# A two-layer decoder trunk on one core: identity products ahead of the last expert block's second half, and block 12's scatter ahead of the last turn

## The reference

```python
for l in range(DEPTH):
    h = rms_norm(x, norm1_g[l]) * (1.0 + sc1) + sh1
    y = even_mixer(...) if l % 2 == 0 else odd_mixer(...)
    x = x + g1 * y
    h = rms_norm(x, norm2_g[l]) * (1.0 + sc2) + sh2
    x = x + g2 * grouped_moe(h, router_w, router_b, moe_w_gu[l], moe_w_down[l])
return rms_norm(x, final_g)

def grouped_moe(...):
    probs = jax.nn.softmax((t @ router_w).astype(jnp.float32), axis=-1)
    ...
    gu = jnp.einsum('td,edf->etf', t, w_gu)
    act = jax.nn.silu(g) * u * gate_dense.T[:, :, None]
    y = jnp.einsum('etf,efd->td', act, w_down)
```

## Time and profile before

| | |
|---|---|
| median of 3 runs | 828.9 us (828.89 to 831.48) |
| profiled execution | 831.04 us, of which 829.2 us are its span |
| TensorE busy | 764.6 us, 92% of the span |
| DVE busy | 358.6 us, 43% |
| ACT busy | 172.6 us, 21% |
| mean granted TensorE clock | 0.986 of full speed |
| HBM read | 292.18 MB, 354 GB/s over the span |
| experts of layer 0 end with | the identity products at 392.9 to 395.8 us |
| experts of layer 1 end with | the last scatter at 818.8 to 820.8 us |

### The profile page before, as it was taken

The page is one execution under the profiler, slowest core; times in us unless marked ns, Lnnn a source line. Parts: engine busy times, 40 slices in busy tenths (PEclk is TensorE's granted clock), DMA queues, the critical chain, the costliest instruction groups (busy, mean ns, idle before and its releaser), DMA issues.

```text
span 829.2 us, 12109 instructions
## 1 busy us (share of the span) xinstructions
PE 764.6 (92%) x4952; PEld 398.7 (48%) x4952; DVE 358.6 (43%) x878; ACT 172.6 (21%) x423; POOL 14.8 (2%) x62
## 2 busy tenths in 40 slices
PE   4999999999999998866999999999999999998764
PEld 2557464464343332322777888864553434333221
DVE  0177982383222212202779957363663321221202
ACT  2033240441111011001300244253431111100101
POOL 2000000000000000000000000000000000000000
PEclk9999999999999999998999999999999999999979
DMA  9999999698999999999999935353978999999993
GB/s 344 389 387 384 386 387 411 272 421 331 416 409 390 432 425 425 427 425 404 386 386 368 330 123 204 128 204 122 385 262 334 424 419 407 423 427 428 429 419 160
DMA packets 67643, 295.12 MB, mean 356 GB/s; under 512 B 3200, under 2 KB 4864, under 8 KB 51968
## 3 DMA queue, kind: packets, MB, share of 16 engines
q1 hardware_dynamic: 65600, 291.16, 88.7%
q10 hardware_dynamic: 1840, 2.62, 0.9%
q0 software_dynamic: 144, 0.52, 0.2%
HBM read 292.18 MB, written 1.05 MB: 354 GB/s over the span
## 4 chain that ended last, share of the span: by engine, by line
PE 51%; issue 21%; DMA 12%; DVE 9%; SPq 4%; ACT 2%; POOL 0%; POOLq 0%; DVEq 0%; ACTq 0%
PE bank L1251 10%; DMA ring<-w_gu_dram 9%; PE bank L885 8%; DVE tail L2161 6%; PE bank L1273 4%; SPq L544 4%; PE bank L881 4%; PE bank L1078 3%; PE bank L1237 3%; PE bank L795 3%; DMA ring<-ada_w_dram 2%; PE bank L771 2%; DVE gb L1804 2%; PE bank L1012 2%; PE bank L1028 2%
## 5 line engine op out<-in xcount | busy, mean ns | idle before, releaser
L1251 PE MATMUL bank<-ring,scr 128*64 128x512 f32 (+1 forms) x992 | 195.4, 627 | 33.0 <-DMA ring<-w_gu_dram 20.5
L885 PE MATMUL bank<-hT,ring 128*128 128x256 f32 x640 | 141.6, 380 | 0.4 <-DVE hT L1892 0.4
L1251 PEld LDWEIGHTS bank<-ring,scr 128*64 128x64 f32 (+1 forms) x992 | 56.4, 132 | 155.3 <-issue 129.0
L885 PEld LDWEIGHTS bank<-hT,ring 128*128 128x128 f32 x640 | 120.6, 190 | 17.6 <-issue 1.6
L1273 PE MATMUL bank<-ring,scr 128*64 128x512 f32 (+1 forms) x544 | 102.4, 597 | 0.4 <-issue 0.4
L1804 DVE SCALAR_TENSOR_TENSOR gb<-ring,small,gb 128x512 f32<-128x512 f32 x84 | 63.2, 752 | 2.9
L881 PE MATMUL bank<-ring,hT 128*128 128x512 f32 x128 | 56.9, 598 | 0.6 <-ACT hT L1509 0.5
L2383 DVE SCALAR_TENSOR_TENSOR hT<-bank,small,gb 128x512 f32<-128x512 f32 x26 | 19.5, 751 | 87.2 <-PE bank L1273 85.7
L1273 PEld LDWEIGHTS bank<-ring,scr 128*64 128x64 f32 (+1 forms) x544 | 29.3, 127 | 54.9 <-issue 52.7
L2370 DVE TENSOR_TENSOR hT<-bank,hT 128x256 f32<-128x256 f32 x28 | 11.9, 424 | 83.9 <-ACT hT L1731 83.9
L2161 DVE SCALAR_TENSOR_TENSOR tail<-scr,col,tail 128x256 f32<-128x256 f32 x120 | 47.7, 474 | 0.0
(11 more groups left out here) (318 smaller groups left out, 772.1 us busy)
## 6 DMA issues: line engine op xcount, KB each, us to landing
ring<-w_gu_dram SPq DMA_DIRECT2D x58, 2048.0 KB, 19.0
ring<-w_down_dram SPq DMA_DIRECT2D x28, 2048.0 KB, 15.1
ring<-ada_w_dram SPq DMA_DIRECT2D x24, 2048.0 KB, 15.9
ring<-od_w_in_dram SPq DMA_DIRECT2D x9, 2048.0 KB, 19.9
ring<-ev_w_in_dram SPq DMA_DIRECT2D x5, 2048.0 KB, 19.6
ring<-w_down_dram SPq DMA_DIRECT2D x8, 1024.0 KB, 27.6
scr<-w_gu_dram SPq DMA_DIRECT2D x12, 512.0 KB, 10.7
ring<-ev_w_out_dram SPq DMA_DIRECT2D x2, 2048.0 KB, 18.2
```

The lines of the kernel that those rows point to most:

```text
L885: ins = pe.matmul(banks[h][:, m * 256:(m + 1) * 256], w[:, c, (2 * h + m) * P:(2 * h + m + 1) * P], x_part[:, c, :], start=(c == 0 and m = ...
L1251: ins = pe.matmul(b[o:o + r, :].rearrange("p (u f) -> p u f", u=2), h[:, c, r * i:r * i + r], wm, start=(first and c == 0), stop=(last and ...
```

## The change

It changes three places in the experts of both layers. On TensorE, in the loop's last round (b = 13), three identity products into bank 0 stand between the turn of the slot map and `up(13, 1)`. Behind the loop, `scatter(12)` stands ahead of `turn_act(13)` instead of behind it. On DVE, `low_y(12)` stands ahead of `activation(13)` instead of behind it. No wait, no load and no buffer is new.

```diff
@@ -1399,11 +1399,13 @@
                     if b % 2 == 1 or b == BLOCKS - 1:
                         pe.wait_ge(pg_built, built(l, b // 2))
                         slots_T(fill_t("PT", b // 2), pg[b // 2 % 2], range(2 if b % 2 else 1)).then_inc(t_full, 1)
+                    if b == BLOCKS - 1:
+                        keep_busy(3, bank[0])
                     up(b, 1)
                     if b == 0:
                         rows_of(b)
+                scatter(BLOCKS - 2)
                 turn_act(BLOCKS - 1)
-                scatter(BLOCKS - 2)
                 result(BLOCKS - 1)
                 scatter(BLOCKS - 1)
                 if l == 0:
@@ -2431,8 +2433,8 @@
                         slot_map(pcur[SLOTS_AT[b] % 2], rgs, SLOTS_AT[b])
                 slots_out(BLOCKS // 2 - 1)
                 result(BLOCKS - 2)
+                low_y(BLOCKS - 2)
                 activation(BLOCKS - 1)
-                low_y(BLOCKS - 2)
                 dve.wait_ge(flag_ready, l + 1)
                 over = dve.value_load(flag[0:1, l:l + 1])
                 result(BLOCKS - 1)
```

## The result

The changed kernel takes 833.4 us (median of 22 runs), the kernel before, beside it, 829.9 (22 runs): a ratio of 1.0032, with a 95% interval from 1.0021 to 1.0043. The means, from which the ratio comes, differ by 2.7 us (833.1 and 830.4), the medians by 3.5. Forecast were 828.8 and a range of 827.6 to 831.2. Of the distance from 828.8 to 833.4, 1.0 us is the kernel before itself, whose median over 22 runs is 829.9 where the three runs that the forecast started from gave 828.9. The profiled execution took 831.69 us, 829.9 of it span, with a mean granted TensorE clock of 0.983.

The account below looks back on a forecast made before the run. The prediction took weight landings by DMA to bound each layer's expert end. Layer 1 gained 0.0 and layer 0 was taken as 0, so the 828.9 us median less 0.1 gave 828.8, range 827.6 to 831.2.

Parts of the forecast that it names:

- The bound: End of each layer's experts: the last down products' second half starts when its weights land, so earlier work gains little.
- The 2.25 us won in layer 1: Layer 1's end: TensorE's 2.25 us gain becomes a 2.2 us wait for the last down weights; gain 0.0 us.
- the copy: ACT's copy of the turned activations, formerly hidden by the scatter, now delays the down products: some 0.5 us with handover.
- the low part on DVE: Block 12's low part, 0.68 us, runs before the last multiplication on DVE and costs nothing, with 4 us in hand.
- the first rival: Slower: the wait inside the last down products lets the clock fall; 1.8 to 2.8 us in layer 1; chances 0.14 and 0.05.
- Clock falls in the new wait, in the median of executions: one layer 0.14, both 0.05: Chances that TensorE's clock falls in the 2.2 us wait inside the last down products: 830 to 831.6, or up to 833.
- the 0.7 won: Layer 0's end: the last down products' second half starts at 387.4 instead of 388.2, so the layer ends 0.7 us sooner.
- That chain hangs on a landing, not on TensorE: Layer 1's mixer: DVE and ACT work after ada_w lands sets TensorE's turn, so TensorE 0.7 us sooner waits 0.7 longer.
- layer 0's gain: Layer 0's experts end 0.7 us sooner, but the next mixer absorbs it: worth 0 to 0.7 us, taken as 0.
- the 0.8 us of slack: Layer 0's end: the last down weights land at 387.39, 0.8 us before the down products' second half starts at 388.2.
- The faster rival: Landings move along with TensorE: layer 0 gives 3.2 us, layer 1 2.2, total 823.5; chance 0.06 in full or over half.
- The rival of products that miss their gap: Weights come before the identity products end; up to 2.8 us lost but swallowed by layer 1's slack and the mixer; 0.01.

Follow-up runs that it names:

- e3: The changed kernel plus two identity products in the wait between the halves of the last down products: 829.2 us, ratio 0.9982 against the kernel before.
- e12: The changed kernel plus three identity products between the halves of the last down products: 831.6 us, ratio 1.0020 against the kernel before.
- e8: The changed kernel itself, run again as a control: 832.8 us, ratio 1.0036 against the kernel before.
- e5_layer1_only: The change in layer 1 alone, layer 0 with TensorE's old order and no products, DVE's order changed in both: 831.1 us, ratio 1.0014.
- e9: The changed kernel plus two identity products between the halves of the last down products, measured again in another set: 829.6 us, ratio 0.9999.
- e7: The changed kernel with block 12's scatter moved between the halves of the last down products, one identity product behind it: 830.1 us, ratio 1.0000.
- e11: The changed kernel with block 12's scatter and one identity product between the last down halves, measured again in another set: 829.25 us, ratio 0.9995.

## Why the prediction was wrong

**Right, by its own steps.** The bound: the second half of the last down products starts at the landing of the last weights (815.97 before, 814.22 with the change, 816.97 in e3; only in e12, whose fill is too long, 0.4 us behind it), and from there to the end of the span it is 13.2 us wherever the clock holds. The 2.25 us won in layer 1 did become a wait, of 2.27 us against 2.2 forecast. The products fit their gap, the second half of up took 3.64 us, the copy was exposed for 0.47 us against 0.5, the low part on DVE cost nothing. The mechanism of the loss was the first rival, in its place, and its price for layer 1 was 1.8 to 2.8 us; measured 2.4.

**Wrong: the step "Clock falls in the new wait, in the median of executions: one layer 0.14, both 0.05".** The forecast gave this rival 0.19 in all; by the mean clock it came in 23 of 34 runs, and the median run of the change, at 833.4 us, is one of them. It was weighed by comparing 2.2 us with the delays after which the clock had fallen before (2.2 and 2.9 us), as if the fall had to come before work resumes. In the change's profile it comes 1.2 us after work resumed, in layer 1, and not at all in layer 0 of the same execution behind a longer wait. In the three cases seen the fall came 3.1 to 3.5 us after TensorE had stopped and 0.7 to 1.2 us into the work, so a wait shorter than the delay did not protect. The delay also varies more than the two values that were weighed: in the kernel before TensorE stands 6.17 and 6.28 us ahead of block 13's first half (until 362.75 and 791.43), and there the clock fell 5.4 and 3.5 us after the stop (at 361.9 and 788.6). Every fall of the trace of before lay inside a gap, so that trace could not show one behind a wait; but it showed no gap of 2 us that had been forgiven, only some of 1.24 us and the like, and that should have carried at least even odds. The Trainium skill's sentence on bursts parted by waits for DMA ("TensorE: Matmul & The Clock Gate", "HAM oscillation — how this bites in real kernels") pointed the right way for most executions, but not in how it happens: here the burst behind the wait started at full clock and lost it 0.7 to 1.2 us in, and behind three of the six profiled waits it kept it. The section tells of a kernel whose waits are longer than 2.3 us. The same page, in "Why this matters for your kernels", warns only of idle gaps longer than that too; three of this case's waits of 2.27 to 2.37 us were followed by a fall, so there the traces disagree.

**The price of a fall: two errors that cancel.** In both layers the rival counted 1.8 us for the second half, as if all of it ran low, and the last scatter (1.99 us more, if wholly low) only in part. Measured: 0.64 and 1.79 us in layer 1, 1.10 and 1.76 in layer 0, since the fall came inside the second half and lasted through the whole scatter. The totals, 2.4 and 2.9 us, lie in and just above the 1.8 to 2.8 of the forecast; in layer 0, less the 0.7 won, 2.2 against "1 to 2". That they fit is in part luck.

**True only of the execution that was read: "That chain hangs on a landing, not on TensorE".** The forecast took layer 0's gain as worth 0, because the first class turn in the mixer waits for ACT. These lines of TensorE's weight load for that turn, before and with the change, show who comes last:

```profile
486.12 0.42 PEld L729 LDWEIGHTS bank<-ident,scr 128*128 128x128 f32 x4 [0.50 <-ACT scr L1640]
```

```profile
484.57 0.57 PEld L729 LDWEIGHTS bank<-ident,scr 128*128 128x128 f32 x4
```

With the change there is no wait for ACT: TensorE is the late one. In 13 of the 14 profiles the turn starts 86.40 or 86.41 us after the mixer's first products (398.38 and 484.79 with the change, 401.48 and 487.88 in e8); only in that of before it is 86.67. So the chain over DVE and ACT came last in the execution that the forecast read, and in none of the others. In that execution DVE's wait for ada_w ended 33.7 us behind the landing of the last down weights; in e12_three_products it ended 32.4 us behind it (419.42 and 387.02). Why it was late there is not shown. The page's chain of the work that ended last says the same, before and then with the change:

```profile
PE 51%; issue 21%; DMA 12%; DVE 9%; SPq 4%; ACT 2%; POOL 0%; POOLq 0%; DVEq 0%; ACTq 0%
```

```profile
PE 63%; issue 21%; DMA 11%; DVE 2%; ACT 1%; POOL 0%; SPq 0%; DVEq 0%; POOLq 0%; ACTq 0%
```

Where TensorE comes last, what layer 0 loses up to its last down products is paid in full, and what it wins is kept as long as TensorE stays last. The landing of ada_w does not set the turn there: with the change DVE's wait for it ended here,

```profile
419.35 0.48 DVE L1803 TENSOR_SCALAR gb<-ring,small 128x512 f32<-128x512 f32 x1 [4.78 <-DMA ring<-ada_w_dram]
```

and in e5_layer1_only, with layer 0's old program on TensorE, here:

```profile
418.81 0.49 DVE L1806 TENSOR_SCALAR gb<-ring,small 128x512 f32<-128x512 f32 x1 [4.77 <-DMA ring<-ada_w_dram]
```

In e8 it ended at 419.66, 0.3 us behind the first of these, and the turn was 3.1 us late.

**Not settled: how large layer 0's gain is.** The second half starts 0.8 us behind its weights in the profile of before, but in e5, with the same program for layer 0 but for DVE's order, it waits 0.32 us for them. So the 0.8 us of slack that the forecast used is one draw, and the gain is between 0 and 0.8 us from execution to execution. Landings differ by 2 us between executions whatever the kernel (ada_w 418.7 to 421.1), more than the gain, and no kernel whose wait is covered is below the one before in both of its sets (e3 0.9982 and e9 0.9999; e7 1.0000 and e11 0.9995).

**The faster rival** found no support. **The rival of products that miss their gap** is not what happened: in the profiles the second half of up starts 0 to 1.5 us behind the products.

## What to carry to other kernels

Work that is made earlier in front of a fixed landing turns into idle time, and on TensorE idle time of 2 us is not free: it can put the work behind it, which sets the end, at half the clock. Before filling one gap, ask where the time reappears; either leave it where a low clock is hidden, as the kernel before does, or cover the new wait as well, with no more than it holds. And one execution shows one draw of when the clock falls and of which chain comes last: look at several, and count executions by their mean granted clock, rough as that is, before giving a fall a small chance.

## What the runs showed of the hardware

The clock's fall need not lie in the idle time: three times it came 0.7 to 1.2 us after TensorE had resumed, in the midst of back-to-back products, and the low level then lasted 6.8 us in layer 0 (388.0 to 394.9) through work without a gap over 0.9 us. Waits of 2.27 and 2.38 us in one execution ended one with a fall and one without; of six such waits in four profiles three had a fall behind them. With 1.98 us of products in that wait no run of 24 had a mean clock under 0.986; with 1.1 us of them 3 of 24 had, which shows no more than that a fall may have come.
